# Two norms from one set of sums: the joints between projections in the second block of a two-block transformer

## The chip, the cores and the metric

One core of one Trainium2 chip. The metric is the device time of one execution in microseconds (us); three runs of the kernel before took 1743.28, 1743.62 and 1748.15. TensorE multiplies matrices, VectorE (DVE) and ScalarE (ACT) do the elementwise work, SyncE (SP) issues the loads. TensorE's weights stand in `SBUF` tiles; its results go to eight PSUM banks, here `PA` (four) and `PB` (four).

## The reference

Two blocks run one after the other on 256 tokens (16 more in the first block) of width 1024. The change touches the second block alone, which has two layers, and 256 context tokens beside the 256 of the sequence. Layer 1 needs the context only as keys and values.

```python
def rms_norm_2(x, g):
    y = xf * lax.rsqrt(jnp.mean(xf * xf, axis=-1, keepdims=True) + EPS)
    return (y * g.astype(jnp.float32)).astype(x.dtype)
def modulate(x, g, shift, scale):
    return rms_norm_2(x, g) * (1 + scale) + shift
...
    for layer in range(DEPTH):
        with_ctx = layer < DEPTH - 1
        sh_m, sc_m, gt_m, sh_f, sc_f, gt_f = ada_chunks(c, w_ada[layer], b_ada[layer])
...
        xm = modulate(h, g_pre_m, sh_m, sc_m)
...
        h = h + gt_m * rms_norm_2(y, g_post_m)
        f = conv_ffn(modulate(h, g_pre_f, sh_f, sc_f), w_up[layer], conv_w[layer], conv_b[layer], w_down[layer])
        h = h + gt_f * rms_norm_2(f, g_post_f)
        if with_ctx:
            hc = hc + cgt_m * rms_norm_2(yc, g_post_m)
...
```

So between two projections stand a norm of the output y (the norm behind), the update h + gain * norm(y), and a norm of the new h (the norm in front of the next projection).

## The kernel before

Activations are kept transposed: eight tiles k of 128 features, each with T columns, one per token; T is 512 in layer 0 (half v = 0 the sequence, half v = 1 the context, 256 columns each) and 256 at the end of layer 1. `H2` holds h, `YV` holds y. A projection is computed in split precision: weights come from HBM into a ring of four 1 MB slots (`raw`), ScalarE writes their high part `WH` (`split_hi`, L2066), VectorE the low part `WL` (`split_lo`, L1437), and each output tile is three matmuls per k: WH x high, WH x low, WL x high (L850). The input's parts are `XH` and `XL`. A split frees its slot and is made as soon as the place of an old tile is free; those of a projection's last tiles are deferred into the norm behind it.

The order of work is written out by hand as a list, `plan`, which every engine walks in order; semaphores keep the engines together. `four_tiles` (L913, L914, L923) computes the first four output tiles of a projection k by k, as inputs come, and half by half (its `parts`), and the products with `WL` at the end of each half.

A norm behind (`Norm` of kind post) collects squares in `acc` while the writing projection's tiles come (ScalarE squares at L2102, VectorE adds at L1448), sums over the features by matmuls with ones (`quarter_sums`, L982), takes root (L2247) and reciprocal (L1578), spreads the row over all partitions into `PA` (L975) and copies it to `rt` (L2254). `update_dve` then scales each tile and half (L1630) and adds pairs of tiles into h (L1637); `update_act` squares these pairs (L2290), `pair_sums` sums them, and the norm in front goes through the same root, spread and copy before it scales (L1594), rounds to `XH` (L2269) and subtracts to `XL` (L1604). `halves` plans this per half; in front of layer 1's q projection (2 x 2 tiles q, then q2, then kv with both halves) the second half's squares and root are placed among q's matmuls (`inner`).

The modulation's own projection w_ada is spread over the program in 1 MB pieces: `ada_sums` is eight matmuls (L791) on one ring slot, which they free. `fill` says at which places of a norm TensorE does the held pieces: `start`, `sum`, `end`, or `k0` to `k3` behind a pair of squares. On ScalarE every fourth piece copies out a row (L2087), every block a few columns (L2076).

## Time and profile before

| | us |
|---|---|
| median of three runs | 1743.62 |
| lowest, highest | 1743.28, 1748.15 |
| profiled execution | 1750.94 |
| its span, first to last instruction | 1748.7 |
| TensorE busy | 1622.7 (93%) |
| VectorE busy | 1014.4 (58%) |
| ScalarE busy | 843.6 (48%) |
| mean granted TensorE clock | 0.967 |

The profile is of one execution, and the times of single instructions come from it. Busy shares are over the whole span; what a stretch is worth is seen in the chain of waits and in windows of it. TensorE's clock has two levels, 2.4 GHz (granted clock 1.0) and 1.2 GHz (0.5).

### The profile page before, as it was taken

The numbers are of one execution on the slowest core, as the hardware profiler recorded it, in microseconds if no ns is written. First come the engines' busy times: TensorE is split into PE (matmuls) and PEld (weight loads), VectorE is DVE, ScalarE is ACT, GpSimd is POOL, SyncE is SP. The second block draws the span as 40 slices with busy tenths as digits, with TensorE's granted clock in tenths as the row PEclk, the third lists the DMA queues.
The fourth block names the chain that finished last, engine by engine and source line by source line (L and its number), as shares of the span: only waits on it lengthen the run. The fifth ranks groups of instructions, "written<-read, shape, count | busy, mean of one in ns | idle before, by whom it ended". The sixth has DMA issues, their size and how long they took to land.

```text
span 1748.7 us, 27458 instructions
## 1 busy us (share of the span) xinstructions
PE 1622.7 (93%) x11494; PEld 1418.3 (81%) x11494; DVE 1014.4 (58%) x1621; ACT 843.6 (48%) x1410; POOL 21.1 (1%) x38
## 2 busy tenths in 40 slices
PE   6978999989898999999989899999999698989997
PEld 6947999989577999887758678888887574779997
DVE  7675645465856555724463665425553766577576
ACT  6744534448445444534463454324432537556563
POOL 0000000000000000220000000000000000000000
PEclk9989999999898999999999899999999899989998
DMA  7455546353455464772202442232223430244642
GB/s 286 145 175 189 207 141 217 124 192 144 167 214 197 141 234 133 211 223 82 87 1 73 169 170 97 83 129 88 83 82 137 181 109 25 73 182 151 230 143 91
DMA packets 60523, 253.84 MB, mean 145 GB/s; under 512 B 4977, under 2 KB 8305, under 8 KB 42481
## 3 DMA queue, kind: packets, MB, share of 16 engines
q1 hardware_dynamic: 59088, 248.95, 40.2%
q0 software_dynamic: 1312, 3.15, 1.0%
q8 instruction: 91, 1.49, 0.3%
q14 instruction: 32, 0.25, 0.0%
HBM read 251.03 MB, written 1.05 MB: 144 GB/s over the span
## 4 chain that ended last, share of the span: by engine, by line
PE 63%; DVE 3%; ACT 2%; issue 1%; DVEq 0%; ACTq 0%
PE PA L850 48%; PE PA L913 2%; PE PA L914 2%; PE PB L1209 2%; PE PA L923 1%; PE PB L1196 1%; PE PB L791 1%; DVE tmp L1630 1%; PE PA L1393 1%; PE PA L1281 1%; PE PA L886 1%; PE PA L887 1%; PE PA L892 1%; PE PB L982 1%; ACT tmp L2470 1%
## 5 line engine op out<-in xcount | busy, mean ns | idle before, releaser
L1437 DVE TENSOR_TENSOR WL_t<-raw,WH_t 128x1024 fp32r<-128x1024 f32 (+1 forms) x344 | 444.7, 1298 | 361.7 <-ACT WH_t L2066 361.4
L850 PE MATMUL PA<-XH_t,WH_t 128*128 128x256 f32 (+2 forms) x1984 | 631.9, 318 | 8.4 <-issue 4.4
L850 PE MATMUL PA<-XL_t,WH_t 128*128 128x256 f32 (+2 forms) x1984 | 626.1, 316 | 0.0
L850 PE MATMUL PA<-XH_t,WL_t 128*128 128x256 f32 (+2 forms) x1984 | 625.7, 315 | 0.0
L2066 ACT ACTIVATE WH_t<-raw 128x1024 fp32r<-128x1024 f32 (+1 forms) x344 | 381.4, 1113 | 208.8 <-PE PA L850 171.1
L850 PEld LDWEIGHTS PA<-XH_t,WH_t 128*128 128x128 f32 x1984 | 379.2, 191 | 40.6 <-issue 15.0
L850 PEld LDWEIGHTS PA<-XH_t,WL_t 128*128 128x128 f32 x1984 | 379.3, 191 | 21.5
L850 PEld LDWEIGHTS PA<-XL_t,WH_t 128*128 128x128 f32 x1984 | 379.4, 191 | 21.4 <-issue 0.5
L850 PE MATMUL PA<-AH_t,WH_t 128*128 128x256 f32 (+2 forms) x616 | 192.0, 312 | 0.3 <-DVE AL_t L1460 0.2
L850 PE MATMUL PA<-AH_t,WL_t 128*128 128x256 f32 (+2 forms) x616 | 190.8, 310 | 0.0
L850 PE MATMUL PA<-AL_t,WH_t 128*128 128x256 f32 (+2 forms) x616 | 190.3, 309 | 0.0
L1522 DVE SCALAR_TENSOR_TENSOR tmp<-PA,par,tmp 128x510 f32<-128x510 f32 (+1 forms) x88 | 53.7, 614 | 122.6 <-ACT tmp L2192 122.6
L2192 ACT ACTIVATE tmp<-PA,par 128x512 f32<-128x512 f32 (+1 forms) x88 | 58.5, 668 | 136.3 <-PE PA L850 124.6
L850 PEld LDWEIGHTS PA<-AH_t,WL_t 128*128 128x128 f32 x616 | 115.7, 188 | 6.8
L850 PEld LDWEIGHTS PA<-AH_t,WH_t 128*128 128x128 f32 x616 | 115.7, 188 | 6.7 <-DVE AL_t L1460 0.9
L850 PEld LDWEIGHTS PA<-AL_t,WH_t 128*128 128x128 f32 x616 | 115.5, 188 | 6.5
L2146 ACT ACTIVATE big<-PA 128x272 f32<-128x272 f32 (+2 forms) x72 | 33.0, 461 | 134.3 <-PE PA L850 120.7
L913 PE MATMUL PA<-XH_t,WH_t 128*128 128x256 f32 (+1 forms) x288 | 85.0, 325 | 12.7 <-DVE XL_t L1604 7.6
L914 PE MATMUL PA<-XL_t,WH_t 128*128 128x256 f32 (+1 forms) x288 | 82.7, 317 | 0.0
L913 PEld LDWEIGHTS PA<-XH_t,WH_t 128*128 128x128 f32 x288 | 65.4, 227 | 17.1 <-issue 11.0
L914 PEld LDWEIGHTS PA<-XL_t,WH_t 128*128 128x128 f32 x288 | 65.3, 227 | 0.0
L791 PE MATMUL PB<-raw,cpad_t 128*32 128x256 f32 x768 | 56.9, 422 | 0.0
(262 smaller groups left out, 1644.7 us busy)
## 6 DMA issues: line engine op xcount, KB each, us to landing
raw<-in_w_ada SPq DMA_DIRECT2D x48, 1024.0 KB, 5.2
raw<-in_w_gu SPq DMA_DIRECT2D x44, 1024.0 KB, 4.8
raw<-in_w_dn SPq DMA_DIRECT2D x64, 704.0 KB, 4.1
raw<-in_w_up SPq DMA_DIRECT2D x44, 1024.0 KB, 4.8
raw<-in_w_in SPq DMA_DIRECT2D x30, 1024.0 KB, 5.0
raw<-in_w_out SPq DMA_DIRECT2D x12, 1024.0 KB, 4.8
raw<-in_w_qkv SPq DMA_DIRECT2D x6, 1024.0 KB, 6.0
raw<-in_w_outc SPq DMA_DIRECT2D x4, 1024.0 KB, 5.8
```

Source lines behind the costliest of these rows:

```text
L791: mm = pe.matmul(ada_psum[b // 6][0][32 * j:32 * j + 32, :], cpad[:, k, :], RAWV[:, r % RAW, c:c + 256], start=(k == 0), stop=(k == 7))
L850: mm = pe.matmul(PA[:, (L.b0 + o) % 4, 0:T], W[:, c:c + P], X[:, k, L.x0:L.x0 + T], start=(n == 0 and m == 0 and not L.early), stop=(n == ...
L886: pe.matmul(PA[:, bank, 0:L.T], WH_t[:, c:c + P], hi[:, k, 0:L.T], start=(k == 0), stop=False)
L887: pe.matmul(PA[:, bank, 0:L.T], WH_t[:, c:c + P], lo[:, k, 0:L.T], start=False, stop=False)
L913: pe.matmul(PA[:, bank % 4, a:b], WH_t[:, c:c + P], hi[:, k, a:b], start=(k == 0), stop=False)
L914: pe.matmul(PA[:, bank % 4, a:b], WH_t[:, c:c + P], lo[:, k, a:b], start=False, stop=False)
L1209: mm = pe.matmul(PB[64 * c:64 * c + 64, v % 2, 0:256], value(v, c, kb), a_PT(second, v % 2)[c][:, j, :], start=(j == 0), stop=(j == len(bl ...
L1437: dve.tensor_tensor(WL_t[:, w:w + L.cols], RAWV[:, r % RAW, part * UNIT:part * UNIT + L.cols], WHf[:, w:w + L.cols], ALU.subtract).then_in ...
L1522: dve.scalar_tensor_tensor(c[:, :, 1:SEQ], ps[:, :, 0:SEQ - 1], tap(o, 0), c[:, :, 1:SEQ], ALU.mult, ALU.add).then_inc(S("conv_left"), 1)
L2066: act.activation(WH_t[:, w:w + L.cols], RAWV[:, r % RAW, part * UNIT:part * UNIT + L.cols], ACT.Copy).then_inc(S("w_hi"), 1)
L2146: act.activation(L.dst[:, k, 0:T], PA[:, (L.b0 + o) % 4, 0:T], ACT.Copy).then_inc(S("of_act"), 1)
L2192: act.activation(conv[s % 2][x][:, 0:T], PA[:, (L.b0 + o) % 4, 0:T], ACT.Identity, bias=biasv(L.layer)[:, bass.ds(c, 1)], scale=tapv(L.lay ...
```

## The change

In three places of the second block (behind the output projection of layer 0's mixer, behind layer 0's feed-forward part and behind the output projection of layer 1's mixer) the two norms and the update between them become one step, `Joint`. With r the reciprocal root of y's mean square and yg = gain * y, the new mean square is the mean of h^2 + 2 r h yg + r^2 yg^2. While the writer's tiles come, ScalarE makes y^2, yg and yg^2 (`tail_gain`), VectorE h * yg (`tail_product`), and adds the three side by side (`tail_sum`); the sum of h^2 is carried from step to step in `arow`. TensorE sums over features in `PB` (`add`) and spreads both roots there by matmuls with one row of the identity; VectorE reads them from `PB` without a copy. Update, norm and low part go over pairs of tiles (512 columns); scale and shift are applied by ScalarE, once into `XH` and once into a float copy `j_xf`. The last norm of the program stays as it was.

With it, held pieces of w_ada stand behind k = 1, 3, 5 or 7 of a half (`k03` is half 0, k = 3), the first four splits of q2's weights and the copies out of q's banks are made in the second half's loop, and the head operations of layer 1 start two tiles later (squares and rotation of the first heads with q2's tiles 1 and 2 instead of 0).

TensorE, behind the mixer of layer 0, before: `tmp` is `acc` or squares of h, `raw` a piece of w_ada, `spread` and `cboth` constants.

```order
L791 MATMUL PB<-raw,cpad_t 32x256 x7
L982 MATMUL PB<-tmp,cboth 32x128 [waits n_rt,n_acc]
L982 MATMUL PB<-tmp,cboth 32x128 x3
L791 MATMUL PB<-raw,cpad_t 32x256 [waits raw_loaded1]
L791 MATMUL PB<-raw,cpad_t 32x256 x7
L975 MATMUL PA<-tmp,spread 128x128 [waits of_act,n_rc]
L975 MATMUL PA<-tmp,spread 128x128 x3
L791 MATMUL PB<-raw,cpad_t 32x256 [waits raw_loaded2]
L791 MATMUL PB<-raw,cpad_t 32x256 x7
L982 MATMUL PB<-tmp,cboth 32x64 [waits n_sq,n_rt]
L982 MATMUL PB<-tmp,cboth 32x64 x7
```

The same place with the change (line numbers are those of the changed file; L828 is the piece of w_ada, L977 a sum, L1000 a root's spread, L950 the first matmul behind the gap).

```order
L977 MATMUL PB<-tmp,cboth 32x128 [waits j_d]
L977 MATMUL PB<-tmp,cboth 32x128 x3
L977 MATMUL PB<-tmp,cboth 32x256 [waits j_b,j_c]
L977 MATMUL PB<-tmp,cboth 32x256 x3
L813 MATMUL PB<-cboth,big 128x128 [waits ada_free,ada_row]
L813 MATMUL PB<-cboth,big 128x128
L828 MATMUL PB<-raw,cpad_t 32x256 [waits raw_loaded0,ada_row]
L828 MATMUL PB<-raw,cpad_t 32x256 x7
L1000 MATMUL PB<-tmp,cboth 128x2x64 [waits j_rc]
L1000 MATMUL PB<-tmp,cboth 128x2x64 x3
L1000 MATMUL PB<-tmp,cboth 128x2x64 [waits j_rc]
L1000 MATMUL PB<-tmp,cboth 128x2x64 x3
```

Of four pieces in this gap two are left, and both roots follow each other with no squares of the new h between them.

VectorE in the same place, before: one half's first four tiles of the norm in front.

```order
L1594 SCALAR_TENSOR_TENSOR tmp<-H_t,mod,tmp 128x256 [waits n_cp]
L1594 SCALAR_TENSOR_TENSOR tmp<-H_t,mod,tmp 128x256
L1604 SCALAR_TENSOR_TENSOR XL_t<-tmp,ada,XH_t 128x256 [waits n_hi]
L1594 SCALAR_TENSOR_TENSOR tmp<-H_t,mod,tmp 128x256 x2
L1604 SCALAR_TENSOR_TENSOR XL_t<-tmp,ada,XH_t 128x256 [waits n_hi]
L1594 SCALAR_TENSOR_TENSOR tmp<-H_t,mod,tmp 128x256 [waits x_ready]
L1604 SCALAR_TENSOR_TENSOR XL_t<-tmp,ada,XH_t 128x256 [waits n_hi]
```

And with the change: L1720 is the norm of a pair, L1707 the next pair's product, L1715 its update, L1728 the low part, L1485 a weight split.

```order
L1720 TENSOR_TENSOR tmp<-H_t,PB 128x512 [waits dve_chain,j_sum]
L1707 TENSOR_TENSOR tmp<-Y,PB 128x512
L1715 TENSOR_TENSOR H_t<-H_t,tmp 128x2x256 [waits dve_chain]
L1728 TENSOR_TENSOR XL_t<-tmp,XH_t 128x2x256 [waits j_x]
L1485 TENSOR_TENSOR WL_t<-raw,WH_t 128x1024 [waits w_hi]
L1720 TENSOR_TENSOR tmp<-H_t,PB 128x512 [waits dve_chain]
L1707 TENSOR_TENSOR tmp<-Y,PB 128x512
L1715 TENSOR_TENSOR H_t<-H_t,tmp 128x2x256 [waits dve_chain]
L1728 TENSOR_TENSOR XL_t<-tmp,XH_t 128x2x256 [waits j_x]
```

The update, which stood ahead of the whole norm, now stands inside it, and the deferred split behind the first low part instead of ahead of the updates.

TensorE between the pairs of the first half of q's tiles (layer 1), where nothing but matmuls of q and one sum stood before:

```order
L951 MATMUL PA<-XL_t,WH_t 128x256
L828 MATMUL PB<-raw,cpad_t 32x256 [waits raw_loaded3]
L828 MATMUL PB<-raw,cpad_t 32x256 x7
L950 MATMUL PA<-XH_t,WH_t 128x256 [waits x_ready]
L951 MATMUL PA<-XL_t,WH_t 128x256
```

A piece of w_ada, with its wait for a load, now stands ahead of q's next pair.

```diff
+                self.ahead = 4 if lead and len(parts) < len(lead.halves) else 0
...
-                px, pc = halves(last_post, l, both)
-                q = linear("copy", w_qkv, 2, SEQ, XV, None, dst=prj2, held=6, parts=[(0, SEQ, tiles_ready(px))], inner=pc)
-                left = last_post.fill(q.slots(), act=2, start=1, sum=1)
-                pc.fill(px.fill(left, k0=1), end=3)
-                q2 = linear("copy", w_qkv, 2, SEQ, XV, tiles_ready(px), dst=prj2, tile0=4)
-                q2.beside, q2.scaled = ("heads", 0), tiles_ready(pc)(KD - 1)
-                kv = linear("copy", w_qkv, 2, T2, XV, tiles_ready(pc), dst=prj2, tile0=8)
+                j = Joint(0, G_FFN, 1, A_MIX, 0, last)
+                q = linear("copy", w_qkv, 2, SEQ, XV, None, dst=prj2, held=6, parts=[(0, SEQ, j.ready(0))], lead=j)
+                j.fill(q.slots(), 2, 4, sum=1, end=1, k01=1, k03=1, k05=1, k07=1)
+                q2 = linear("copy", w_qkv, 2, SEQ, XV, j.ready(0), dst=prj2, tile0=4)
+                q2.beside, q2.scaled = ("heads", 0), j.ready(1)(KD - 1)
+                kv = linear("copy", w_qkv, 2, T2, XV, j.ready(1), dst=prj2, tile0=8)
...
+            j = Joint(l, G_MIX, l, A_FFN, 24, w)
+            up, last = ffn(l, T, "conv", w_up2, w_dn2, YV, None, held=(6, 4)[l], ada=(4, 0)[l],
+                           mods=(1, 5, 6) if l else (1, 0, 2), lead=j,
+                           parts=[(a, a + SEQ, j.ready(v)) for v, a, *_ in j.halves])
             if l == 0:
-                p[1].fill(p[0].fill(post.fill(up.slots(), start=1, sum=1, end=1), k1=1), end=2)
+                j.fill(up.slots(), 2, 2, sum=1, end=1, k03=1, k07=1, k13=1, k15=1)
             else:
-                p[0].fill(post.fill(up.slots(), start=1, end=1), k1=1, end=1)
-            groups = [(0, SEQ, (l, 0, G_FFN), None), (SEQ, T2, (l, 1, G_FFN), None)][:T // SEQ]
-            last_post = norm([w], "post", l, T, YV, groups, direct=False)
-            writers = [last_post]
+                j.fill(up.slots(), 2, 2, sum=1, end=1, k03=1, k05=1)
+        last_post = norm([last], "post", l, T, YV, [(0, SEQ, (l, 0, G_FFN), None)])
...
+                        if L.lead:
+                            norm_slots_pe(L.lead, f"k{v}{k}")
...
+            def joint_pe(J):
+                V = len(J.halves)
+                def add(x, b, nb, start, stop):
+                    for j in range(4):
+                        mm = pe.matmul(PB[32 * j:32 * j + 32, 3 if b else 0, 64 * V * b:64 * V * (b + nb)].rearrange(
+                            "p (s h t) -> p s h t", s=nb, h=V), ones[:, 0:32],
+                            x[:, b:b + nb, :].rearrange("p s (h j t) -> p s j h t", j=4, t=SEQ // 4)[:, :, j],
+                            start=start, stop=stop, skip_group_check=True)
+                    return mm
+                pe.wait_ge(S("j_acc"), J.acc0 + KD - 2)
+                add(products(J.T, 0), 0, 1, True, False)
+                add(products(J.T, 0), 1, 2, True, False)
+                last = products(J.T, 2)
+                pe.wait_ge(S("j_d"), J.d0 + KD)
+                add(last, 0, 1, False, True).then_inc(S("j_sum"), 1)
+                pe.wait_ge(S("j_c"), J.c0 + KD)
+                pe.wait_ge(S("j_b"), J.b0 + KD)
+                add(last, 1, 2, False, True).then_inc(S("j_sum"), 1)
+                norm_slots_pe(J, "sum")
+                for r in range(2):
+                    pe.wait_ge(S("j_rc"), 3 * J.n + 2 * r + 1)
+                    for j in range(4):
+                        one = ident[:, 32 * j:32 * j + 1].to_broadcast([P, P])
+                        mm = pe.matmul(quarter(PB[:, (0, 3)[r], 0:J.T], j), one,
+                                       j_r[r][:, 0:64 * V].rearrange("p (h t) -> p h t", h=V), start=True, stop=True)
+                    mm.then_inc(S("j_sum"), 1)
+                norm_slots_pe(J, "end")
...
+            def tail_sum(J, k):
+                if not 0 < k < KD - 1:
+                    return
+                dve.wait_ge(S("j_c"), J.c0 + k + 1)
+                dve.wait_ge(S("j_b"), J.b0 + k + 1)
+                if k > 1:
+                    dve.wait_ge(S("j_acc"), J.acc0 + k - 1)
+                s = products(J.T, 0)
+                dve.tensor_tensor(s, s, products(J.T, 1 + k % 2), ALU.add).then_inc(S("j_acc"), 1)
+            def tail_product(J, k):
+                name, value = J.yg(k)
+                dve.wait_ge(S(name), value)
+                if k > 2:
+                    dve.wait_ge(S("j_acc"), J.acc0 + k - 2)
+                dve.tensor_tensor(products(J.T, 1 + k % 2 if k else 0)[:, 1, :], H2[:, k, 0:J.T], YV[:, k, 0:J.T],
+                                  ALU.mult).then_inc(S("j_b"), 1)
...
+            def joint_dve(J):
+                V = len(J.halves)
+                g0, w = 2 * J.n, 64 * V
+                updated = {}
+                r, r2, t = (x[:, 0:w] for x in j_r)
+                dve.wait_ge(S("j_rt"), g0 + 1)
+                dve.reciprocal(r, r).then_inc(S("j_rc"), 1)
+                def product(g):
+                    v, p = divmod(g, 4)
+                    link(dve.tensor_tensor(j_m[g % 2], YV[:, 2 * p:2 * p + 2, SEQ * v:SEQ * v + SEQ], joint_root(0, v),
+                                           ALU.mult))
+                def update(g):
+                    v, p = divmod(g, 4)
+                    h = H2[:, 2 * p:2 * p + 2, SEQ * v:SEQ * v + SEQ]
+                    count[0] += 1
+                    updated[g] = count[0]
+                    dve.tensor_tensor(h, h, j_m[g % 2], ALU.add).then_inc(S("dve_chain"), 1)
+                def normed(g):
+                    v, p = divmod(g, 4)
+                    dve.wait_ge(S("dve_chain"), updated[g])
+                    dve.tensor_tensor(j_hn[g % 2], H2[:, 2 * p:2 * p + 2, SEQ * v:SEQ * v + SEQ], joint_root(1, v),
+                                      ALU.mult).then_inc(S("j_hn"), 1)
+                def low(g):
+                    v, p = divmod(g, 4)
+                    dve.wait_ge(S("j_x"), J.x0 + g + 1)
+                    k, c = slice(2 * p, 2 * p + 2), slice(SEQ * v, SEQ * v + SEQ)
+                    dve.tensor_tensor(XL[:, k, c], j_xf[g % 2], XHf[:, k, c], ALU.subtract).then_inc(S("x_ready"), 1)
+                dve.wait_ge(S("j_rc"), 3 * J.n + 1)
+                dve.wait_ge(S("j_sum"), 4 * J.n + 2)
+                link(dve.tensor_tensor(t, joint_rows(2, V), r, ALU.mult))
+                link(dve.scalar_tensor_tensor(t, joint_rows(1, V), 2.0, t, ALU.mult, ALU.add))
+                link(dve.tensor_tensor(t, t, r, ALU.mult))
+                link(dve.tensor_tensor(t, t, arow[:, 0:w], ALU.add))
+                dve.tensor_scalar(arow[:, 0:w], t, 0.0, None, ALU.max).then_inc(S("j_rc"), 1)
+                dve.wait_ge(S("j_sum"), 4 * J.n + 3)
+                product(0)
+                dve.wait_ge(S("j_rt"), g0 + 2)
+                dve.reciprocal(r2, r2).then_inc(S("j_rc"), 1)
+                update(0)
+                dve.wait_ge(S("j_sum"), 4 * J.n + 4)
+                ahead = [x for o in range(J.host.ahead) for x in J.host.split_early(o)]
+                for g in range(4 * V):
+                    normed(g)
+                    if g + 1 < 4 * V:
+                        product(g + 1)
+                        update(g + 1)
+                    if g > 4 and ahead:
+                        split_lo(*ahead.pop(0))
+                    low(g)
+                    if deferred:
+                        split_lo(*deferred.pop(0))
+                for x in ahead:
+                    split_lo(*x)
...
+            def tail_gain(J, k, ps):
+                pr = products(J.T, 1 + k % 2 if k else 0)
+                if k > 2:
+                    act.wait_ge(S("j_acc"), J.acc0 + k - 2)
+                if k == 0:
+                    act.wait_ge(S("mods"), 1 + J.n)
+                act.activation(pr[:, 0, :], ps if J.copy else YV[:, k, 0:J.T], ACT.Square).then_inc(S("j_d"), 1)
+                if not J.copy:
+                    act.wait_ge(S("j_d"), J.d0 + k + 1)
+                name, value = J.yg(k)
+                for v, a, gain, _, _ in J.halves:
+                    y = YV[:, k, a:a + SEQ]
+                    ins = act.activation(y, ps[:, a:a + SEQ] if J.copy else y, ACT.Copy, scale=modc(*gain, k))
+                ins.then_inc(S(name), 1)
+                act.wait_ge(S(name), value)
+                act.activation(pr[:, 2, :], YV[:, k, 0:J.T], ACT.Square).then_inc(S("j_c"), 1)
...
+            def joint_act(J):
+                V = len(J.halves)
+                w = 64 * V
+                act.wait_ge(S("j_sum"), 4 * J.n + 1)
+                act.activation(j_r[0][:, 0:w], joint_rows(0, V), ACT.Sqrt, bias=eps, scale=1.0 / D).then_inc(S("j_rt"), 1)
+                if deferred:
+                    split_hi(*deferred.pop(0))
+                act.wait_ge(S("j_rc"), 3 * J.n + 2)
+                act.activation(j_r[1][:, 0:w], arow[:, 0:w], ACT.Sqrt, bias=eps, scale=1.0 / D).then_inc(S("j_rt"), 1)
+                while deferred:
+                    split_hi(*deferred.pop(0))
+                for slot, r in J.slots[:J.cp[0]]:
+                    ada_sums(slot, r)
+                ahead = J.host.ahead
+                for v, a, _, gain, shift in J.halves:
+                    for p in range(4):
+                        act.wait_ge(S("j_hn"), J.f0 + 4 * v + p + 1)
+                        x = j_hn[p % 2]
+                        for k in (2 * p, 2 * p + 1):
+                            act.activation(XH[:, k, a:a + SEQ], x[:, k % 2, :], ACT.Identity,
+                                           bias=shiftc(gain[0], shift, k), scale=modc(*gain, k))
+                        for k in (2 * p, 2 * p + 1):
+                            ins = act.activation(j_xf[p % 2][:, k % 2, :], x[:, k % 2, :], ACT.Identity,
+                                                 bias=shiftc(gain[0], shift, k), scale=modc(*gain, k))
+                        ins.then_inc(S("j_x"), 1)
+                        if v and ahead:
+                            L = J.host
+                            act.wait_ge(S("out_ready"), L.tile(0, p // 2, p % 2))
+                            act.activation(L.dst[:, L.tile0 + p, 0:L.T], PA[:, (L.b0 + p) % 4, 0:L.T],
+                                           ACT.Copy).then_inc(S("of_act"), 1)
+                            for y in L.split_early(p):
+                                split_hi(*y)
+                    for slot, r in J.slots[J.cp[0]:J.cp[1]] if v == 0 else []:
+                        ada_sums(slot, r)
+                for slot, r in J.slots[J.cp[1]:]:
...-                if (o, n) == (4, 3):
+                if (o, n) == (4, 5):
                     spread_heads(1)
```

## Rows read from the trace of the kernel before

**Rows 1.** The page: busy us (share) xinstructions, and shares of the chain.
```profile
PE 1622.7 (93%) x11494; PEld 1418.3 (81%) x11494; DVE 1014.4 (58%) x1621; ACT 843.6 (48%) x1410; POOL 21.1 (1%) x38
...
PE 63%; DVE 3%; ACT 2%; issue 1%; DVEq 0%; ACTq 0%
```

**Rows 2.** Windows: stretch, length, busy of PE PEld DVE ACT POOL, clock, DMA, GB/s.
```profile
963.20:979.10 15.90, 8.00 (x156) 4.41 (x153) 10.88 (x20) 7.17 (x14) 0.00 (x0) 0.87 0.67 247
979.10:1010.20 31.10, 31.10 (x302) 28.67 (x306) 19.70 (x45) 13.21 (x26) 0.00 (x0) 0.90 0.29 112
1354.00:1371.10 17.10, 7.83 (x138) 4.33 (x134) 12.51 (x22) 7.89 (x14) 0.00 (x0) 0.80 0.04 7
...
1390.20:1412.10 21.90, 16.18 (x116) 15.21 (x116) 15.89 (x21) 11.62 (x23) 0.00 (x0) 0.92 0.71 278
1527.40:1542.40 15.00, 7.57 (x153) 4.19 (x152) 10.15 (x20) 6.40 (x13) 0.00 (x0) 0.86 0.77 289
1542.40:1556.80 14.40, 14.40 (x97) 14.21 (x97) 7.07 (x17) 6.05 (x11) 0.00 (x0) 0.79 0.28 104
...
1504.10:1527.40 23.30, 23.30 (x198) 23.17 (x200) 12.23 (x20) 13.12 (x24) 0.00 (x0) 1.00 0.34 113
```

**Rows 3.** Chain that ended last, in order of time: start us, us, what.
```profile
919.37 43.85 PE PA L850 x192
...
966.52 0.55 PE PA L975 x8
...
967.73 1.67 DVE tmp L1630 x4
...
979.09 0.55 PE PA L913
...
1010.20 1.00 PE PB L791 x16
...
1456.01 1.11 PE PB L1196 x8
```

**Rows 4.** Groups with shapes apart, 880 to 1560: busy us, mean ns.
```profile
L1437 DVE TENSOR_TENSOR WL_t<-raw,WH_t 128x1024 fp32r<-128x1024 f32 x74 | 90.1, 1221 | 48.8 <-ACT WH_t L2066 48.7
...
L1448 DVE TENSOR_TENSOR tmp<-tmp 128x512 f32<-128x512 f32 x14 | 9.7, 690 | 20.2 <-ACT tmp L2102 20.2
...
L1578 DVE RECIPROCAL tmp<-tmp 128x64 f32<-128x64 f32 x6 | 3.3, 553 | 12.0 <-ACT tmp L2247 12.0
L1448 DVE TENSOR_TENSOR tmp<-tmp 128x256 f32<-128x256 f32 x7 | 3.0, 425 | 2.9 <-ACT tmp L2102 2.9
...
L1578 DVE RECIPROCAL tmp<-tmp 128x128 f32<-128x128 f32 x2 | 1.9, 952 | 1.9 <-ACT tmp L2247 1.9
...
L1705 DVE TENSOR_SCALAR cphase<-cphase,par 128x128 f32<-128x128 f32 x1 | 0.3, 280 | 0.0
...
L2066 ACT ACTIVATE WH_t<-raw 128x1024 fp32r<-128x1024 f32 x75 | 78.6, 1052 | 6.6 <-PE PA L850 5.7 <-DMA raw<-in_w_qkv 0.8 <-PE PA L923 0.2
...
L2269 ACT ACTIVATE XH_t<-tmp,ada 128x256 fp32r<-128x256 f32 x40 | 19.3, 506 | 11.1 <-DVE tmp L1594 11.1
...
L2192 ACT ACTIVATE tmp<-PA,par 128x256 f32<-128x256 f32 x3 | 1.7, 559 | 7.1 <-PE PA L923 7.1
```

**Rows 5.** The chain again in B, then timelines of SP and ScalarE there.
```profile
1390.20 4.45 issue
...
1419.15 1.73 PE PB L1298 x8
...
1369.45 0.37 SPq L718 DMA_DIRECT2D raw<-in_w_ada  x1
...
1383.44 1.06 ACT L2066 ACTIVATE WH_t<-raw 128x1024 fp32r<-128x1024 f32 x1 [0.76 <-DMA raw<-in_w_qkv]
...
1394.18 0.92 ACT L2146 ACTIVATE big<-PA 128x256 f32<-128x256 f32 x3
```

**Rows 6.** Timeline of TensorE behind A's gap: start us, us, instruction.
```profile
979.65 0.41 PE L913 MATMUL PA<-XH_t,WH_t 128*128 128x256 f32 x1
...
985.71 0.28 PE L913 MATMUL PA<-XH_t,WH_t 128*128 128x256 f32 x1
```

More of the change, by code:

```diff
@@ L436, in all_ready, with norm @@
             return lambda k: ("x_ready", v)
-        def halves(post, l, groups):
-            pre = []
-            for v, g in enumerate(groups):
-                post.xn.append(take("n_xn", KD))
-                n = Norm("pre", l, SEQ, H2, [g], direct=True)
-                pre.append(n)
-                plan.append(("update", (post, v, n)))
-                plan.append(("norm", n))
-            return pre
-        def norm(writers, *a, **k):
-            k.setdefault("direct", a[0] == "pre" and a[3] is H2)
-            n = Norm(*a, alone=not writers and not k["direct"], **k)
+        def norm(writers, *a):
+            n = Norm(*a, alone=not writers)
             for w in writers:
@@ L977, in roots_pe @@
                 norm_slots_pe(n, "end")
-            def quarter_sums(w, x, start, stop):
-                for j in range(4):
-                    mm = pe.matmul(PB[32 * j:32 * j + 32, 0, 0:w], ones[:, 0:32], x[:, j * w:(j + 1) * w],
-                                   start=start, stop=stop)
-                return mm
             def lru_gates(l, half):
```

249 lines of the change are left out of this document (126 added, 123 removed).

## The prediction, as written before the result

> **What bounds the kernel now.** I read the page's busy shares and chain first: TensorE is busy 93% of the span and makes up 63% of the chain that ended last, so time can only be won where it waits or runs at half clock [rows 1]. The windows come next. The change touches three places, each between the last tile of one projection and the first ones of the next, called A, B and C: after the mixer of layer 0 (963.2 to 1010.2), after its feed-forward part (1354.0 to 1412.1), and after the mixer of layer 1 (1527.4 to 1556.8). In their gaps of 15.9, 17.1 and 15.0 us TensorE is busy for 8.0, 7.8 and 7.6 us, over half of it the sums of the modulation (L791, below a "slot", 1.0 us each) [rows 2, 3]. The chain goes through it by way of all engines: square, sum, root, reciprocal, spread (966.52), copy, then scaled tiles (967.73) and updates, then a whole second norm until the first matmul at 979.09 [rows 3]. Behind the gap the tiles of 256 columns start at half clock: a matmul starts each 0.21 us at 979.6 and each 0.12 us at 985.7 [rows 6], and the window 979.1 to 1010.2 has a mean granted clock of 0.90 [rows 2]. In B there is a second loss: TensorE stands for 4.45 us at 1390.2, because ScalarE empties the banks of q (L2146) only at 1394.18, behind the second half's norm [rows 5].
>
> **The gap, step by step.** Removed: the spread through `PA` with its copy, eight scalings and four updates of a half, four squares and their sums, and the second root's serial wait. Added: per tile of the writer one more square, a gain in two copies and a square of the result on ScalarE, and a product and a sum over 1536 (C: 768) columns on VectorE.
> In the writers I cost these at nothing. A tile of 512 columns takes 24 matmuls of 43.85/192 = 0.228 us [rows 3], 5.5 us; ScalarE needs 0.6 + 0.8 + 0.6 + 1.05 = 3.1 and VectorE 0.69 + 1.76 + 1.22 = 3.7 (1536 columns by the slope between 512 and 1024) [rows 4]. In C a tile takes 2.87 us (23.3 us for eight tiles [rows 2]); VectorE needs 0.42 + 0.96 + 1.22 = 2.6, so the sum over tiles 0 to 6 ends about 1.4 us behind the last matmul. Were this cover gone, each 0.1 us above 2.87 costs 0.8 us.
> For A, in us of the trace: last matmul out 963.2; square, gained copies, square on ScalarE to 965.1; root to 965.4; reciprocal of 128 columns 0.95 to 966.35 [rows 4]. TensorE meanwhile does the last sums, a transposition and one slot, to 967.15, and spreads the first root with eight passes over the full array: L1196, the nearest row, is 1.11 [rows 3] (ends: 0.55, the old spread L975, and 2.2 at half clock). Five small linked operations of 128 columns at 0.28 + 0.06 [rows 4] (up to 0.42 + 0.06) end at 968.05. Product 0.69, reciprocal 0.95, update 0.62, spread of the second root: 971.1. Then norm 0.69, four affine operations on ScalarE, low part 0.69. The four are my largest unknown: the row with bias alone (L2269) gives 0.506, the one with scale and bias (L2192) 0.559 [rows 4]; started each 0.45 they take 1.93. First matmul at 974.6 instead of 979.1.
> The Trainium skill (ScalarE: Activation LUTs, section "Step-by-step: what each stage is for") calls the scale and bias a free affine step before the lookup. The rows disagree by 0.05 us per operation; were it free, each pair below would take 0.25 us less and the total gain would be about 3 us more.
> B by the same steps, with an addition of 0.69 first, the gain in place, and a copy of a finished row (L2226) that ScalarE makes ahead of its first pair, after the slot at the gap's end: first matmul at 1367.0 instead of 1371.1. C has half the columns (reciprocal 0.55) but the late sum: 1537.5 instead of 1542.4.
>
> **Behind the gap.** The slots are not gone. Six, six and four are held in A, B and C before and after; of those in the gap (four, three, four) two stay, the others move between matmuls.
> New is the pace at which pairs of tiles come. VectorE's order is norm(g), product(g+1), update(g+1), low(g); low waits for ScalarE's four operations. So a pair takes 0.69 + 0.03 + 1.93 + 0.03 + 0.61 = 3.3 us (bounds 3.05 with the 0.40 pace of L2269, 3.55 with four times 0.559), against two tiles in about 1.6 before. TensorE needs 16 x 0.12 = 1.9 us for a pair, so the fast feed becomes the slow one; half clock and slots are hidden under it. A deferred weight split behind low(0) adds 1.2. Pairs of the first half are ready at 0, 4.5, 7.8, 11.1 after the first.
> A: the fourth pair ends at 13.0, a slot at 14.0; ScalarE copies its row only then (14.4) and starts the second half: pairs ready at 17.05, 20.35, 23.65, 26.95. The last ends at 28.85 and the low-weight part (32 x 0.12) at 32.7. 974.6 + 32.7 + 0.4 for half clock in the spread = 1007.7, against 1010.2: **2.5 us**.
> B: two splits are deferred, the second now behind low(1), so the load of the third slot's data is issued at about 5.6 after the first matmul (1372.6, before at 1369.45 [rows 5]). At that row's pace (issue 1369.45, fourth megabyte awaited until 1383.44 [rows 5], 2.6 us each) it lands 6.2 later, at 11.8, and TensorE, in whose queue the slot now stands between pairs, waits some 3 us for it. Slots and pairs then end at 18.6, the low-weight part at 22.5. ScalarE empties q's banks between pairs of the second half and VectorE splits the next weights there, so the 4.45 us goes; q2's tiles start at 24.85, 28.65, 31.5, and, behind the rotation (1.7) and head sums, 38.1, end 41.0: 1408.0 against 1412.1. Less 0.3 for the row spread two steps later in the next tile and 1.0 for half clock after the DMA wait: **2.8 us**.
> C: fourth pair ends at 13.0, low-weight part at 16.85, plus 0.5 for clock: 1554.85 against 1556.8: **1.95 us**.
> Sum 7.2 us. The profiled execution took 1750.94 us with a span of 1748.7, 2.2 outside; it is 0.4% above the median of the runs, 1743.62, and I take the 7.2 us off that median: **1736.4**. A change below 0.3%, 5.2 us, can't be told from none here.
> Bounds of the unknowns: pace 3.05 to 3.55 over 7, 5 and 3 steps, about +-3.5 us; spreads two per place, -3 to +6; clock 0 to 1.9 back; DMA in B +-2. All favourable 1727, all unfavourable 1747.
>
> **Rivals.**
> 1. *TensorE stays the bound.* If ScalarE's and VectorE's steps overlap better than I reckon (a pair in under 2.5), the places shrink to TensorE's own work: A is 974.6 + 192 x 0.12 + four slots = 1001.7 (8.5 less), C 1537.5 + 96 x 0.12 + two = 1551.0 (5.8 less), B, whose DMA wait stays, perhaps 5 less: 19.3 in all, 1724.3. For it: the 31.1 us behind A's gap hold square sums of the second half, which go. Against it: low(g) can't start before four operations of 0.5 us.
> 2. *Half clock.* TensorE, fed 1.9 us of work per 3.3 us, is not granted the full clock again while it is fed so. Then slots and low-weight parts run at half pace: 3.84 more in each of four low-weight parts less what the wait hides (2), 0.9 in some four slots: +12 on the forecast, 1748.4, no change or just slower. For it: the clock fell in gaps where TensorE was half busy, 0.80 to 0.87 [rows 2]. Against it: at half clock a pair (3.4) plus slot (1.9) is more than the feed, so the engine has no idle time then, and without idle time it got the full clock back at 985 [rows 6]. The Trainium skill (TensorE: Matmul & The Clock Gate, section "HAM oscillation — how this bites in real kernels") says that waits between groups of matmuls throttle the array again and each group then starts cold; no row here shows short waits of 1.4 us doing it.
> 3. *Slower: the exchange between VectorE and ScalarE.* A pair is one ring: norm, four affine, low. Some 15 such steps stand on the path. Each 0.1 us per pair costs 1.5 us: at 3.8 the gain is gone, at 4.1 it is slower by 0.3%, and without any overlap (0.69 + 1.93 + 0.62 + 0.69 + 0.62 = 4.6) it costs 19 us, 1756. For it: four buffers of two are shared and each link waits for completion. Against it: the order puts product and update under ScalarE's 1.93.
> 4. *The shorter gap buys nothing*, since the feed gives it all back: 2 us less than now, 1741.6.
>
> **Chances.** Forecast 0.50, rival 1 0.13, rival 2 0.10, rival 3 0.07, rival 4 0.20. The forecast's own range is 1732 to 1740; about a fifth of its chance lies above 1738.4. Faster: 0.40 + 0.13 + a share of rival 4 = 0.60; same 0.31; slower 0.09 (rival 3 and the tail of 2). Range 1727.5 to 1743.5.
>
> **What would show it.** The first matmul behind each gap 4 to 5 us earlier than now; pairs of x each 3.3 us, with TensorE idle before them for VectorE; in B a wait for the load of in_w_ada inside the pairs, no 4.45 us before q2. The forecast is wrong if VectorE's low parts come in under 2.8 or over 3.8 us, if the writers' tiles take longer than 5.5 and 2.87, or if the matmuls of the pairs start each 0.21 us for more than the first two pairs.

## The result, and the profile after

| | before | changed |
|---|---|---|
| runs of the first comparison, median us | 1745.06 (5) | 1751.4 (5) |
| ratio, 95% interval | | 1.0035 (1.0019 to 1.0051) |
| second comparison, more runs, median us | 1749.06 (35) | 1755.42 (12) |
| ratio, 95% interval | | 1.0025 (1.001 to 1.004) |
| profiled execution, its span | 1750.94, 1748.7 | 1749.56, 1747.7 |

Of the 35 runs of before one, at 3401.61 us, is a slow run and left out of the ratios. The ratios are those on record and not quotients of the medians (for the second comparison that would be 1.0036).

The change makes the kernel slower by about 0.3%, some 5 us. 1736.4 was forecast, with a range up to 1743.5: wrong in sign. The two profiled executions hide it: that of before is above all its timed runs, that of the changed kernel among the lowest of its own. So the traces are compared place by place, and a second trace of each kernel (e1, e5) stands beside the first.

The page of the changed kernel, busy times, in the columns of [rows 1]:

```profile
PE 1625.0 (93%) x11230; PEld 1415.2 (81%) x11230; DVE 1033.8 (59%) x1598; ACT 872.2 (50%) x1469; POOL 21.0 (1%) x38
```

Windows of the changed kernel, columns as in [rows 2]: A's gap and what is fed behind it, the last tiles of B's writer, B's gap and all behind it to kv's second tile, C's gap and its fed part (the part behind the gap, in which TensorE is fed with pairs).

```profile
960.80:972.88 12.08, 6.83 (x84) 3.91 (x83) 8.63 (x16) 5.71 (x12) 0.00 (x0) 0.86 0.00 1
972.88:1006.84 33.96, 30.72 (x262) 26.86 (x266) 19.64 (x30) 17.73 (x34) 0.00 (x0) 0.95 0.59 217
1326.90:1352.68 25.78, 24.51 (x104) 18.86 (x102) 14.83 (x14) 10.95 (x16) 0.00 (x0) 1.00 0.33 123
1352.68:1371.60 18.92, 9.34 (x81) 4.88 (x81) 11.92 (x19) 7.06 (x13) 0.00 (x0) 0.73 0.15 56
1371.60:1421.75 50.15, 43.64 (x325) 36.13 (x325) 35.53 (x43) 29.01 (x53) 0.00 (x0) 0.93 0.59 231
1526.30:1537.09 10.79, 6.00 (x81) 3.85 (x81) 8.05 (x17) 4.85 (x10) 0.00 (x0) 0.79 0.15 56
1537.09:1555.40 18.31, 17.69 (x126) 15.53 (x127) 9.11 (x14) 9.02 (x17) 0.00 (x0) 0.75 0.75 287
```

And two stretches of before that were not shown, with the same work: the last tiles of B's writer, and from B's first matmul to kv's second tile.

```profile
1330.27:1353.95 23.68, 23.68 (x108) 19.17 (x110) 9.48 (x10) 6.34 (x7) 0.00 (x0) 1.00 0.41 143
1371.10:1421.45 50.35, 43.73 (x379) 37.73 (x379) 34.95 (x57) 24.87 (x45) 0.00 (x0) 0.93 0.60 229
```

Read with [rows 2]: A's gap fell from 15.9 to 12.1 us, C's from 15.0 to 10.8, but B's rose from 17.1 to 18.9; and the last tiles of B's writer, where TensorE was never idle before, take 25.8 us instead of 23.7, with 1.3 us of it idle. The fed parts grew: A 31.1 to 34.0, C 14.4 to 18.3 at a granted clock of 0.75.

What happens in B's writer is seen in the timelines of ScalarE and VectorE over one tile (start, us, engine, line, operation, idle time before it and what ended that). L1549 adds tile k into y, L2252, L2259 and L2262 are square, gain and square, L2205 and L1485 the high and low weight split, L1518 the product and L1509 the sum over 1536 columns:

```profile
1338.79 0.68 DVE L1549 TENSOR_TENSOR Y<-Y,PA 128x512 f32<-128x512 f32 x1
...
1343.17 1.63 DVE L1485 TENSOR_TENSOR WL_t<-raw,WH_t 128x1408 fp32r<-128x1408 f32 x1 [3.69 <-ACT WH_t L2205]
1344.71 0.68 DVE L1518 TENSOR_TENSOR tmp<-H_t,Y 128x512 f32<-128x512 f32 x1
1345.49 1.76 DVE L1509 TENSOR_TENSOR tmp<-tmp 128x1536 f32<-128x1536 f32 x1
1347.16 0.68 DVE L1549 TENSOR_TENSOR Y<-Y,PA 128x512 f32<-128x512 f32 x1
```
```profile
1339.56 0.63 ACT L2252 ACTIVATE tmp<-Y 128x512 f32<-128x512 f32 x1 [4.86 <-issue]
1340.22 0.91 ACT L2259 ACTIVATE Y<-Y,mod 128x256 f32<-128x256 f32 x2
1341.17 0.63 ACT L2262 ACTIVATE tmp<-Y 128x512 f32<-128x512 f32 x1
1341.70 1.36 ACT L2205 ACTIVATE WH_t<-raw 128x1408 fp32r<-128x1408 f32 x1
```

Each engine is idle about half the time, and yet the tile takes 1347.16 - 1338.79 = 8.37 us: addition, ScalarE's three operations and its split, the low split, product and sum form one ring, in which one engine always waits for the other. TensorE needs 33 matmuls of 0.229 = 7.56 us for such a tile. It starts three tiles 0.5, 0.8 and 0.8 us late (by the starts of the same matmuls in both traces), waiting for `WL`, and behind the last tile it waits for the sum:

```profile
PE PB L977 <- DVE tmp L1509: 3.3, 1, 3.3
PE PB L828 <- DMA raw<-in_w_ada: 3.2, 1, 3.2
```

(waits of the changed kernel between 1355 and 1425: engine, tile and line, releaser, us in total, times, longest.) The second row is the forecast wait for the third piece of w_ada.

In A the pairs came as forecast. VectorE's low parts (L1728), all of one form:

```profile
976.51 0.69 DVE L1728 TENSOR_TENSOR XL_t<-tmp,XH_t 128x512 fp32r<-128x512 f32 x1 [0.83 <-ACT tmp L2414]
...
979.95 0.69 DVE L1728 TENSOR_TENSOR XL_t<-tmp,XH_t 128x512 fp32r<-128x512 f32 x1 [0.82 <-ACT tmp L2414]
...
983.38 0.69 DVE L1728 TENSOR_TENSOR XL_t<-tmp,XH_t 128x512 fp32r<-128x512 f32 x1 [0.82 <-ACT tmp L2414]
```

A pair each 3.43 us, VectorE idle 0.82 of them behind ScalarE's four operations.

All traces by place, in us. A and C: from the start of the writer's last matmul to that of the last low-weight matmul behind the pairs; B: from there to kv's second tile (the 24 matmuls of 512 columns of the first tile and the sums L1352 stand ahead of this point; an expectation below calls it the fifth tile). Behind B stands the attention of layer 1, which the change does not touch.

| | A | gap of A | B | gap of B | C | gap of C |
|---|---|---|---|---|---|---|
| before | 47.1 | 16.3 | 67.9 | 17.6 | 29.4 | 15.3 |
| before, e5 | 47.0 | 16.9 | 68.9 | 17.3 | 27.8 | 15.8 |
| changed | 46.1 | 12.5 | 69.5 | 19.3 | 29.5 | 11.1 |
| changed, e1 | 46.1 | 12.5 | 72.0 | 19.3 | 29.5 | 11.0 |
| e2 sum behind addition | 46.1 | 12.5 | 67.1 | 14.1 | 29.5 | 11.0 |
| e3 norm a pair ahead | 42.5 | 12.5 | 69.0 | 18.1 | 27.6 | 11.1 |
| e4 both | 42.5 | 12.5 | 65.1 | 15.7 | 27.6 | 11.2 |
| e9 e4 + split in gap | 42.2 | 12.8 | 61.2 | 15.7 | 27.5 | 11.2 |
| e10 e4 + row later | 42.5 | 12.5 | 64.1 | 14.4 | 27.6 | 10.9 |
| e6 e4 + both of these | 42.2 | 12.8 | 59.8 | 14.2 | 26.4 | 11.2 |
| e7 e6 + slots in gap | 41.7 | 12.8 | 60.5 | 14.9 | 25.2 | 11.2 |
| e8 changed + slots in gap | 46.1 | 12.5 | 70.3 | 19.3 | 27.8 | 10.8 |

The writers of A and C did not change: from the start of the first to that of the last of their 192 matmuls, 43.4 us in A and 23.0 in C, in both traces of each kernel. Only B's did.

### The profile page after: what moved, and what is told of

It is laid out like the page before. It is cut to its first block and busy times, and to the rows that moved or that the text cites. A ratio compares the mean times of both kernels' runs of the same rounds, so it can differ in the third digit from the quotient of the medians.

```text
span 1747.7 us, 26958 instructions
## 1 busy us (share of the span) xinstructions
PE 1625.0 (93%) x11230; PEld 1415.2 (81%) x11230; DVE 1033.8 (59%) x1598; ACT 872.2 (50%) x1469; POOL 21.0 (1%) x38
## 5 line engine op out<-in xcount | busy, mean ns | idle before, releaser
L1485 DVE TENSOR_TENSOR WL_t<-raw,WH_t 128x1024 fp32r<-128x1024 f32 (+1 forms) x344 | 444.5, 1297 | 359.9 <-ACT WH_t L2205 359.4
L2205 ACT ACTIVATE WH_t<-raw 128x1024 fp32r<-128x1024 f32 (+1 forms) x344 | 380.8, 1111 | 170.0 <-PE PA L887 141.8
L950 PE MATMUL PA<-XH_t,WH_t 128*128 128x256 f32 (+1 forms) x288 | 86.5, 329 | 16.4 <-DVE XL_t L1728 11.5
L950 PEld LDWEIGHTS PA<-XH_t,WH_t 128*128 128x128 f32 x288 | 65.4, 227 | 27.1 <-issue 16.4
L828 PE MATMUL PB<-raw,cpad_t 128*32 128x256 f32 x768 | 59.9, 436 | 3.2 <-DMA raw<-in_w_ada 3.2
```

Of the source, the lines that this page charges most:

```text
L828: mm = pe.matmul(ada_psum[b // 6][0][32 * j:32 * j + 32, :], cpad[:, k, :], RAWV[:, r % RAW, c:c + 256], start=(k == 0), stop=(k == 7))
L950: pe.matmul(PA[:, bank % 4, a:b], WH_t[:, c:c + P], hi[:, k, a:b], start=(k == 0), stop=False)
L1485: dve.tensor_tensor(WL_t[:, w:w + L.cols], RAWV[:, r % RAW, part * UNIT:part * UNIT + L.cols], WHf[:, w:w + L.cols], ALU.subtract).then_in ...
L2205: act.activation(WH_t[:, w:w + L.cols], RAWV[:, r % RAW, part * UNIT:part * UNIT + L.cols], ACT.Copy).then_inc(S("w_hi"), 1)
```

## The experiments

The timed ones:

| | ratio to before | 95% interval |
|---|---|---|
| e1 changed kernel again | 1.0025 | 1.001 to 1.004 |
| e2 | 0.9992 | 0.9976 to 1.0007 |
| e3 | 0.9984 | 0.9969 to 0.9999 |
| e4 | 0.9963 | 0.9946 to 0.9979 |
| e9 | 0.9931 | 0.9917 to 0.9945 |
| e10 | 0.9938 | 0.9924 to 0.9952 |
| e6 | 0.9912 | 0.9897 to 0.9927 |
| e7 | 0.9911 | 0.9894 to 0.9927 |

e1 to e4 ran on one chip beside each other; differences between them in us are differences of these ratios times 1749.06. By the medians of the twelve runs, e2, e3 and e4 lie 8.1, 9.7 and 10.2 us below e1, where the ratios give 5.8, 7.2 and 10.8; so such a difference is known to about 3 us. e6, e7, e9 and e10 were timed on other chips, and are compared with e4 by way of before.

**e1, the changed kernel again.** No edit.

> The changed kernel once more, unedited, beside the three below and against the kernel before. The traces of the two kernels differ along the program by: -2.4 us ahead of place A (start of the program), -1.0 in A, +2.1 in the writer of B, +1.6 in B, -1.4 in the attention of layer 1, +0.1 in C, so without the start +1.4. The timed runs differ by +6. Theory 1 (the places A to C and the writer of B are all there is, and the start varies from run to run): the ratio is 1.001 to 1.003, and the second trace shows the same differences in A, B and C within 0.3 us. Theory 2 (there is a cost outside the three places that the one profiled execution missed): the ratio is again 1.0035 or more, and the second trace shows it as a stretch, outside A to C, that is longer than in the first one.

Measured 1.0025, and a trace of 1755.6 us against 1747.7. A, the writer of B, the gaps and C repeat within 0.1 us. The rest is 1.1 us more ahead of A, 2.4 more in B (there the wait for the load is 4.4 us for 3.2), and 4.2 more between kv and C, where the granted clock differs. Windows of e1, then of the first trace, over the same two pieces of work:

```profile
1454.20:1462.50 8.30, 7.69 (x38) 4.56 (x38) 6.43 (x15) 5.96 (x16) 0.00 (x0) 0.74 0.00 1
1503.50:1509.00 5.50, 4.76 (x29) 2.78 (x29) 0.06 (x1) 2.26 (x5) 0.00 (x0) 0.75 0.00 0
```
```profile
1449.70:1456.40 6.70, 5.80 (x38) 3.48 (x38) 5.92 (x14) 5.71 (x17) 0.00 (x0) 1.00 0.00 1
1496.90:1501.30 4.40, 3.66 (x31) 2.44 (x32) 0.42 (x1) 2.49 (x6) 0.00 (x0) 1.00 0.00 0
```

The whole stretch from kv's second tile to the last tile of C's writer, in before, e5, the changed kernel and e1:

```profile
1421.40:1527.10 105.70, 95.37 (x624) 66.99 (x620) 66.51 (x124) 62.90 (x141) 0.00 (x0) 0.98 0.13 44
1420.00:1524.20 104.20, 93.76 (x623) 66.08 (x620) 66.44 (x124) 62.83 (x141) 0.00 (x0) 1.00 0.13 45
1421.70:1526.00 104.30, 93.84 (x623) 66.09 (x620) 70.42 (x131) 66.47 (x148) 0.00 (x0) 1.00 0.12 44
1425.20:1533.70 108.50, 98.34 (x623) 68.24 (x620) 70.58 (x131) 66.57 (x148) 0.00 (x0) 0.95 0.12 42
```

At a clock of 1.00 both kernels take the same time for it. The ten traces with the change in them took 104.3 (two), 105.7 (three) or 108.4 to 108.5 (five: e1, e2, e3, e9, e10). Before was never seen at 108.4, but it has only two traces, so it is open whether the change makes the low clock there more frequent.

Theory 1's ratio came true, and its 0.3 us held in A, in C and in B's gap, but not in B as a whole; the longer stretch outside the three places is what theory 2 described. What it costs the changed kernel in the mean is not shown. Over e1's twelve runs the time goes from 1748.67 at a mean clock of 0.970 to 1758.44 at 0.962.

**e5, the kernel before again.** No edit, one execution.

> The kernel before, unedited, for a second trace of it. The places A, B, C and the writer of B should take what they took in the first trace: 47.0 us from the last matmul of A's writer to the first slot behind the low-weight part, 67.5 us in B to kv's fifth tile, 33.0 us in C, each within 0.5 us where the granted clock is the same. If they vary by more than 1 us at the same clock, the comparison of single traces does not hold.

A came out at 47.0, as before. B took 1.0 us more, its part behind the gap at a clock of 0.88 instead of 0.93. C took 1.6 us less, with its fed part of 12.3 us at a clock of 0.95, where the first trace has 14.4 at 0.79 [rows 2]:

```profile
1539.95:1552.25 12.30, 12.29 (x97) 12.11 (x97) 7.10 (x17) 6.04 (x11) 0.00 (x0) 0.95 0.27 105
```

So single traces can be compared to 0.1 us where the clock agrees, and by 1 to 2 us a place where it does not.

**e2, the sum behind the addition.**

```diff
-                            if L.tail:
-                                tail_sum(L.tail, s - 1)
                             dve.wait_ge(S("out_ready"), L.tile(i, s, q))
...
                                               ALU.add).then_inc(S("of_dve"), 1)
+                            if L.tail:
+                                tail_sum(L.tail, s - 1)
```

> One edit: in the writer of B, VectorE sums the products of tile k-1 behind its addition of tile k instead of ahead of it. Theory (a ring in the writer): addition 0.68, ScalarE's square, gain and square 2.1, high split 1.36, low split 1.63, product 0.68 and sum 1.76 follow one another, 8.37 us a tile with their links, where TensorE needs 7.56; the sum now lies beside ScalarE's work, the ring is 6.6, the waits of TensorE for WL (0.5, 0.8, 0.8) go, and the last sum is done earlier, so its wait of 3.3 us at the first sum falls to about 1.3: 3.5 to 4 us less than the changed kernel. Rival (the sum would only be late elsewhere: the load of in_w_ada in B sets the end anyway): 2 us or less.

Measured: 5.8 us less than the changed kernel (1.0025 - 0.9992), and the intervals don't meet. VectorE now adds a tile each 7.55 us, waiting for TensorE and not the reverse:

```profile
1338.17 0.69 DVE L1547 TENSOR_TENSOR Y<-Y,PA 128x512 f32<-128x512 f32 x1 [0.94 <-PE PA L887]
1338.77 1.75 DVE L1509 TENSOR_TENSOR tmp<-tmp 128x1536 f32<-128x1536 f32 x1
...
1345.72 0.69 DVE L1547 TENSOR_TENSOR Y<-Y,PA 128x512 f32<-128x512 f32 x1 [0.94 <-PE PA L887]
```

The same work in another order costs nothing. The tiles give back 2.1 us and the gap 5.2 (19.3 to 14.1). The windows of that gap in e2 and then in e4, which has this edit too, to compare with 1352.68:1371.60 of the changed kernel:

```profile
1353.24:1366.93 13.69, 5.69 (x80) 3.76 (x81) 10.41 (x17) 7.17 (x13) 0.00 (x0) 1.00 0.20 76
1349.56:1364.84 15.28, 7.27 (x81) 4.75 (x81) 11.10 (x18) 8.15 (x16) 0.00 (x0) 0.88 0.19 68
```

Of the 5.2 us, 3.1 are the addition of the last tile: it starts at once behind the last matmul, where the sum had held it back for 3.2 us (1352.68 to 1355.87). The rest goes with the granted clock, 1.00 in this gap against 0.73 in all three traces of the changed order (after, e1, e8); in e4 the clock is 0.88 and the gap 15.7. Then the pairs give some of it away again, at TensorE's wait for the load:

```profile
PE PB L828 <- DMA raw<-in_w_ada: 4.8, 1, 4.8
```

The ring is shown; the rival is right in so far as B as a whole keeps only 2.4 of the 5.2 us against the first trace of the changed kernel (4.9 against e1). Of the 2.8 given away 1.6 are the longer wait; behind the gap the clock is 0.87 instead of 0.93.

**e3, the norm one pair ahead.**

```diff
+                normed(0)
                 for g in range(4 * V):
-                    normed(g)
                     if g + 1 < 4 * V:
                         product(g + 1)
                         update(g + 1)
+                        normed(g + 1)
```

> One edit: VectorE makes product, update and norm of pair g+1 ahead of the low part of pair g, so that ScalarE always has the next pair waiting. Theory (the exchange between VectorE and ScalarE sets the pace, 3.43 us a pair): the pace falls to VectorE's own work, 0.69 + 0.69 + 0.62 + 0.61 = 2.6 to 2.7 us, 0.8 less for each of 6, 5 and 3 pairs; with what the load in B and half clock in C keep, 6 to 10 us less than the changed kernel. Rival (TensorE sets the pace as soon as pairs come faster, since it runs at half clock, 3.4 us a pair): 3 us less or nothing. Rival (the first low part comes later, because three operations stand ahead of it): the first matmul of each place comes 0.7 us later or more, and half of the gain goes.

Measured: 7.2 us less than the changed kernel. Low parts in A come each 2.65 us, back to back with VectorE's other work:

```profile
977.48 0.69 DVE L1728 TENSOR_TENSOR XL_t<-tmp,XH_t 128x512 fp32r<-128x512 f32 x1
...
980.13 0.68 DVE L1728 TENSOR_TENSOR XL_t<-tmp,XH_t 128x512 fp32r<-128x512 f32 x1
...
982.78 0.68 DVE L1728 TENSOR_TENSOR XL_t<-tmp,XH_t 128x512 fp32r<-128x512 f32 x1
```

A gives 3.6 us, C 1.9, B 0.5: there the load is waited for (3.8 us). The first matmul of A did not move (12.5), so the third theory falls.

**e4, both edits.**

> Both edits together. If they are independent, their gains add: 9.5 to 14 us less than the changed kernel, and below the kernel before by 4 to 8 us. If B's end is set by the load of in_w_ada, the sum is 2 to 3 us less than that.

10.8 us less than the changed kernel, and faster than before by 0.37%. The sum of the two alone would be 13.0; the 2.2 missing are within the intervals, and of the size that the load in B would keep, so whether the two gains add is not settled.

**e6, e9, e10, the gap of B.** In e4 VectorE idles 1.6 us in B's gap, behind update(0), and ScalarE waits to copy a finished row until a slot is through, while its first pair is ready. e6 has both edits, e9 the first alone, e10 the second alone:

```diff
                 update(0)
+                if deferred:
+                    split_lo(*deferred.pop(0))
...
-                for slot, r in J.slots[:J.cp[0]]:
-                    ada_sums(slot, r)
...
                     for p in range(4):
+                        for slot, r in J.slots[:J.cp[0]] if v == 0 and p == 1 else []:
+                            ada_sums(slot, r)
```

> The kernel with both edits (e4), and two more: VectorE makes the first deferred low split while it waits for the second root's spread (it stood behind the first low part, in front of the second pair), and ScalarE copies the finished row of the modulation behind the first pair instead of ahead of it. Theory (what stands on the path in B is ScalarE's wait for the slot, 1.3 us, and then the load of in_w_ada, which is issued behind the second deferred split): first matmul of B 1.3 us earlier, the load issued some 3 us earlier, TensorE's wait for it 3.3 to under 1.5; 2.5 to 4.5 us less than e4. Rival (the split delays the norm of the first pair, since the wait there is 1.6 us and the split 1.2): first matmuls up to 0.5 us later in A and C, 1 us less than e4 at most.

> e4 with only one of the two edits of e6: the first deferred low split stands in the gap, while VectorE waits for the second root's spread, and so the second stands behind the first low part. Theory (TensorE's wait for the load of in_w_ada, 3.3 us in e4, is due to the slot of the ring that the second split frees late): the split ends some 3.8 us earlier, the load with it, the wait goes, B ends 3.3 to 4 us earlier than in e4, and A some 0.3. Rival (ScalarE's wait for the slot ahead of its first pair was the cause of e6's gain in B, 5.3 us in its trace): 1.3 us or less here.

> e4 with only the other edit of e6: ScalarE copies the finished row behind its first pair instead of ahead of it. Theory: the first matmul of B comes 1.3 us earlier, and since pairs and splits follow, so do the load and TensorE's wait for it; B ends 1.3 to 2 us earlier, A and C do not change. Rival (the row edit brings most of e6's gain): 3 us or more.

e6 is 8.9 us below e4, twice the expected; in its trace B gives 5.3 of them, A 0.3 and C 1.2. SyncE issues the load for the third slot when the second deferred split is done. In e4 and then in e9:

```profile
1369.54 1.98 SPq L755 DMA_DIRECT2D raw<-in_w_ada  x3
```
```profile
1363.68 1.47 SPq L755 DMA_DIRECT2D raw<-in_w_ada  x3
```

5.9 us earlier, of which 2.1 is the earlier arrival at B. The wait in e4 is the next row, and in e9 and e6 there is none:

```profile
PE PB L828 <- DMA raw<-in_w_ada: 3.3, 1, 3.3
```

By the traces the split brings 3.9 us in B, as expected, and the row 1.0, just under it; e10's wait for the load stays at 3.4. The timed differences, 5.6 and 4.4 us, agree with that for e9; for e10 they say more than the trace, but such a difference is known to some 4 us either way, so it can't tell 1 from 4. The split did not delay the first pair by more than 0.3 us.

**e7 and e8, a slot back in the gap.**

```diff
-                j.fill(up.slots(), 2, 2, sum=1, end=1, k03=1, k07=1, k13=1, k15=1)
+                j.fill(up.slots(), 2, 2, sum=1, end=2, k07=1, k13=1, k15=1)
...
-                j.fill(up.slots(), 2, 2, sum=1, end=1, k03=1, k05=1)
+                j.fill(up.slots(), 2, 2, sum=1, end=2, k05=1)
```

> The changed kernel with only that move of one slot in A and one in C. If C's gain (4.2 us in the gap, none at its end) went to half clock, where a pair takes TensorE 3.4 us and each slot stands behind it, C ends 1.0 to 1.9 us earlier than in the changed kernel. If it went to the pace of VectorE and ScalarE alone (3.43 us), C and A end within 0.3 us of the changed kernel's.

> e6 with one held piece of w_ada (a slot) moved back from the first half's pairs into the end of the gap, in A and in C, where TensorE waits over 4 us for the first low part. Theory (at the new pace of 2.65 us a pair and a slot, 1.9 + 1.0 us, stand on TensorE's path, at half clock in C 3.4 + 1.9): 1.0 to 1.5 us less in C, 0.3 to 1 in A than e6. Rival (pairs stay bound by VectorE): within 0.3 us in both.

In e8, one execution on the changed kernel, C ends 1.7 us earlier and A not at all. C's fed part, to compare with the last window of the changed kernel (18.31 us, clock 0.75):

```profile
1540.03:1556.90 16.87, 14.32 (x111) 13.04 (x112) 9.14 (x14) 9.04 (x17) 0.00 (x0) 0.90 0.78 311
```

TensorE is busy 14.3 us of it instead of 17.7: in the changed kernel it was the engine that set C's third and fourth pair, with a slot at half clock ahead of each, while in A the pace of 3.43 us hid the slot. The clock over e8's gap was 1.00, not 0.79, so the moved slot and the better clock came together, and which of them gave how much is open. On e6 (e7) the move gives 0.5 in A and 1.2 in C by the traces, which is too little to be seen in the ratio.

## Why the prediction was wrong, step by step

- **The writers cost nothing.** This step failed, in B; in A and C it held (43.4 and 23.0 us, unchanged). I held the busy time of each engine, 3.1 and 3.7 us with the split of 1024 columns in it, against a tile of 5.5. That is the tile of A. B's takes TensorE 7.56 us, its splits are of 1408 columns (1.36 and 1.63 us), and VectorE has the addition (0.68) on top. Even so neither engine is full; what counts is the ring through both, 8.37 us against 7.56. Price: 2.1 us in the tiles and up to 5.2 in B's gap, by e2. The sentence "were this cover gone, each 0.1 us above 2.87 costs 0.8" had the right question, put to the wrong writer, and the sign "if the writers' tiles take longer than 5.5 and 2.87" left B's tile out.
- **B's gap, 13.0 us.** It took 18.9. With the sum behind the addition it took 13.7 in e2, at a clock of 1.00, and 15.3 in e4, at 0.88. Of the 5.9 us missed 3.1 are the late addition, about 2 go with the clock in the gap, and 0.7 are left, as in the gaps of A and C: the chain of small steps was priced well.
- **A and C.** Gaps of 11.4 and 10.1 were forecast, 12.1 and 10.8 came. The fed part of A took 34.0 for 32.7 + 0.4, that of C 18.3 for 17.35; in B kv's first matmul came 40.4 us behind the first one (43.4 in e1), for 41.0, so in the first trace B's miss lies in its gap. A gained 1.0 us instead of 2.5. C lost 0.1 against the first trace of before and 1.7 against the second, instead of a gain of 1.95.
- **The pace of 3.3 us a pair.** Right as a mechanism, 3.43 in size: ScalarE's four operations take 2.08 us, where 1.93 was taken. Seven steps of 0.13 are 0.9 us in A. The two rows that I compared, L2269 and L2192, read different memories (`tmp` and `PA`). The row of the changed kernel that does the work of L2269 with a scale added is the better one, at 0.50 us between starts for 0.40:

```profile
L2411 ACT ACTIVATE XH_t<-tmp,ada,mod 128x256 fp32r<-128x256 f32 x40 | 21.8, 593 | 28.3 <-DVE tmp L1720 28.2
```

The Trainium skill (ScalarE: Activation LUTs, "Step-by-step: what each stage is for") calls scale and bias free, but in its section "What ACT_TABLE_LOAD costs" it prices each such operand that is a value per partition at about 93 ns. The trace agrees with the price: 593 ns with scale and bias, 506 with bias alone [rows 4].
- **The wait for the load in B, 3 us.** Right: 3.2, and 4.4 in e1. It was named, priced and then left in place; e9 shows, on e4, that one deferred split, which could have stood in an idle piece of the gap, was its cause. The 4.45 us ahead of q2 went as forecast, though TensorE still waits 2.2 us there for the low split of q2's weights, and q2's first matmul came 25.2 us behind the first one, for 24.85.
- **Half clock (rival 2).** Not as it was put (and its sum, four times 1.84 and four times 0.9, gives 11, not 12), but part of C and of B's gap. In A TensorE worked 2.7 us of each 3.4 and stood between pairs, and the clock stayed at 1.00 (the two windows below); waits of 0.3 to 1.3 us did not bring it down. Behind the wait of 3.2 us in B it did fall: the next pair's matmuls start each 0.21 us, from 1383.40 to 1385.75. In C the first two pairs and the slot behind them ran at half clock (1537.43 to 1546.69), just not more pairs than the two that my last sign of being wrong allowed. The Trainium skill (TensorE: Matmul & The Clock Gate, "HAM oscillation — how this bites in real kernels") describes a loop whose groups of matmuls are shorter than the waits for data between them, so that the array is throttled again and each group starts cold. The trace agrees on both sides: in A the waits are shorter than the 2.7 us of work, in B the wait is longer than the pair ahead of it (1.9 us).

```profile
976.50:979.95 3.45, 2.72 (x29) 2.39 (x32) 2.58 (x5) 2.08 (x4) 0.00 (x0) 1.00 1.03 392
979.95:983.38 3.43, 2.66 (x28) 1.97 (x17) 2.58 (x5) 2.08 (x4) 0.00 (x0) 1.00 1.08 376
```

- **Rival 3, the exchange.** It was the right kind of mechanism, a ring between VectorE and ScalarE, looked for in the pairs, where it took 3.43 us, and not in the writer, where it took 8.37.
- **The base.** I took the 7.2 us off the median of three runs, 1743.62. Later runs of the same kernel had medians of 1748 to 1749, so some 1 to 5 us of the absolute error lie there, and none of the sign.

The sum: 7.2 us of gain forecast, about 5 of loss measured, 12 in all. By the traces 2.1 lie in the tiles of B's writer, 4.4 to 5.9 in B, 1.5 in A and 2.1 to 3.7 in C, 10 to 13 together. What share of the clock's fall in C and in the attention belongs to the change, and what to chance, stays open. In C before shows it too, at 0.79 in one trace and 0.95 in the other; in the attention before was at 0.98 and 1.00, and half of the traces with the change at 0.95, 4.2 us longer than at 1.00.
